# Between two layers of a decoder trunk: the last squares summed on TensorE, the root taken from the sum, a residual in small pieces, the second norm's sums later, and hT normed behind its last reader

## The reference

```
def rmsnorm(x, g):
    y = x * rsqrt(mean(x * x, axis=-1) + 1e-6)
    return y * g

# layer 0 ends with, and layer 1 ends likewise
y = (concat(o_tok, o_mem) * silu(gate)) @ w_o      # 2048 x 2048
x = x + rmsnorm(y, g_post[0])                      # residual

# layer 1 begins with
h = rmsnorm(x, g_pre[1])
p_shift, q_mem, gate = split(h @ w_in)             # r, k, v, two low-rank inputs, memory queries, gate
```

## Time and profile before

| | |
|---|---|
| median of 3 runs | 1711.69 us (1710.7 to 1712.37) |
| the profiled execution's own time | 1713.43 us |
| its span | 1711.8 us |
| PE busy | 1623.2 us, 95% of the span |
| DVE busy | 1049.7 us, 61% |
| ACT busy | 401.3 us, 23% |
| granted TensorE clock, mean | 0.981 of full speed |

### The profile page before, as it was taken

One profiled execution on the slowest core, in us unless ns is written; L12 is line 12 of the kernel. 1 busy time (PEld: TensorE's weight loads), 2 busy tenths in 40 slices (PEclk: granted clock), 3 DMA queues, 4 the chain that ended last, 5 costly groups with the idle time before them and its releaser, 6 DMA issues.

```text
span 1711.8 us, 27852 instructions
## 1 busy us (share of the span) xinstructions
PE 1623.2 (95%) x9596; PEld 1285.7 (75%) x9596; DVE 1049.7 (61%) x4973; ACT 401.3 (23%) x1002; POOL 160.8 (9%) x295
## 2 busy tenths in 40 slices
PE   7999999899999999989989989999999999999995
PEld 6677776677777777657977867777777777888895
DVE  4887546746465555437872467777777777431755
ACT  2131111101121212211111433333333333221011
POOL 1121112112111121220000000000000000020000
PEclk9999999999999999999999999999999999999998
DMA  9689999999999999995433233333333323374441
GB/s 384 235 335 415 411 406 395 384 396 420 405 401 422 417 419 412 366 379 239 148 141 149 103 101 102 103 103 102 103 109 103 103 78 118 111 272 176 148 148 52
DMA packets 101725, 419.95 MB, mean 245 GB/s; under 512 B 41796, under 2 KB 46288, under 8 KB 91984
## 3 DMA queue, kind: packets, MB, share of 16 engines
q0 software_dynamic: 41680, 218.91, 32.1%
q1 hardware_dynamic: 53256, 187.54, 28.9%
q10 hardware_dynamic: 6648, 11.73, 1.8%
HBM read 405.28 MB, written 12.85 MB: 244 GB/s over the span
## 4 chain that ended last, share of the span: by engine, by line
PE 76%; DVE 9%; ACT 6%; DMA 5%; issue 2%; POOLq 0%; POOL 0%; ACTq 0%; DVEq 0%; SPq 0%
PE psum L743 25%; PE psum L1171 11%; PE psum L812 10%; PE psum L794 6%; PE psum L1034 5%; DMA kvr<-in_cv 3%; PE psum L732 3%; PE psum L781 2%; PE psum L1218 2%; DMA kvr<-in_ck 1%; PE psum L1228 1%; PE psum L754 1%; ACT gT L1777 1%; PE psum L769 1%; DVE kvr L1939 1%
## 5 line engine op out<-in xcount | busy, mean ns | idle before, releaser
L1939 DVE CUSTOM_DVE_ANT_0 kvr<-kvr,arena 128x128 f32<-128x128 f32 x1488 | 323.6, 285 | 114.4 <-DMA kvr<-in_ck 114.0
L743 PE MATMUL psum<-hT,wring 128*128 128x264 f32 x1536 | 364.8, 394 | 0.0
L743 PEld LDWEIGHTS psum<-hT,wring 128*128 128x128 f32 x1536 | 291.9, 194 | 67.8 <-issue 19.8
L1171 PE MATMUL psum<-hT,kvr 128*128 128x264 f32 x1152 | 283.0, 391 | 1.8 <-DVE hT L2267 1.8
L1171 PEld LDWEIGHTS psum<-hT,kvr 128*128 128x128 f32 x1152 | 213.5, 191 | 42.3 <-issue 8.9
L794 PE MATMUL psum<-hT,kvr 128*128 128x264 f32 x512 | 121.5, 388 | 0.0
L1939 DVE DVE_READ_ACCUMULATOR2_ANT arena<- 128x1 f32 x1488 | 120.2, 81 | 0.0
L794 PEld LDWEIGHTS psum<-hT,kvr 128*128 128x128 f32 x512 | 94.8, 190 | 15.8 <-issue 0.9
L677 POOL DMA_DIRECT2D kvr<-in_cv x128 | 67.7, 529 | 377.9 <-PE psum L1034 288.2
L1034 PE MATMUL psum<-kvr,arena 128*32 128x384 f32 x1024 | 98.8, 502 | 4.5 <-DMA kvr<-in_cv 4.5
L677 POOL DMA_DIRECT2D kvr<-in_ck x128 | 67.6, 528 | 216.7 <-issue 216.7
(11 more groups left out here) (433 smaller groups left out, 2318.5 us busy)
## 6 DMA issues: line engine op xcount, KB each, us to landing
kvr<-in_ck POOLq DMA_DIRECT2D x128, 768.0 KB, 11.8
kvr<-in_cv POOLq DMA_DIRECT2D x128, 768.0 KB, 11.4
kvr<-in_wrkv SPq DMA_DIRECT2D x12, 3072.0 KB, 11.9
kvr<-in_wo SPq DMA_DIRECT2D x14, 2048.0 KB, 8.3
wring<-in_wkv SPq DMA_DIRECT2D x12, 2048.0 KB, 11.8
wring<-in_wm SPq DMA_DIRECT2D x8, 2048.0 KB, 12.5
wring<-in_wg SPq DMA_DIRECT2D x8, 2048.0 KB, 12.0
kvr<-in_wg SPq DMA_DIRECT2D x8, 2048.0 KB, 8.8
```

Of the source, the lines that this page charges most:

```text
L743: last = mm(psum[:, m % 2, 0:n], w[:, k, t * P:(t + 1) * P], rhs[:, k, 0:n], start=(k == 0), stop=(k == KT - 1))
L1171: last = mm(psum[:, m % 2, 0:T], w[:, k, t * P:(t + 1) * P], hT[:, k, :], start=(k == 0), stop=(k == KT - 1))
L1939: last = v_.tensor_tensor_reduce(page, page, qb[:, n % 2, h * P:(h + 1) * P], 1.0, 0.0, ALU.mult, ALU.add, S[:, n % 2, j * FH + h:j * FH + ...
```

## The change

Seven edits, all between the layers.

- The squares of the last two tiles are no longer added into `acc0` by DVE. PE adds them in PSUM: one product of ones with `acc0` (tiles 0 to 13) and one with each of the two `sq0` buffers, all accumulated into A.
- The root is taken by ACT directly from A, with 1/D as scale and epsilon as bias (a new two-column tile `eps`), and DVE takes the reciprocal of the root. `rsx` moves to the place of `acc0`. A Sqrt of one `eps` column stands ahead of tile 14 on ACT.
- The residual goes in eight pieces of 1, 1, 2, 2, 2, 4, 2 and 2 row tiles, and ACT signals every row tile of `hT` by itself. `lora_tiles` waits for each k.
- The sums of tile 15 (`output_sums(0, 15)`) move behind the fifth piece. The two steps of the second norm that stood before the residual move behind it. The three sums on PE for the second norm move into `lora_tiles`, behind k = 13.
- The low-rank tiles go to PSUM banks 6 and 7, so that the first two query tiles need not wait for their eviction.
- `hT` is multiplied by the second inverse root while the fourth query tile is computed: rows 0 to 3 when that tile has passed k = 3, and so on, and rows 12 to 15 when it is done. Its eviction comes behind that.
- Counts of `h_out` follow (SP's wait ahead of the `s0` loads becomes 28), and the late units' semaphores take the names of `g_full`, which frees names for the new ones.

```
+        RESIDUAL = [(0, 1), (1, 2), (2, 4), (4, 6), (6, 8), (8, 12), (12, 14), (14, 16)]
+        SUMS_LEFT = 5
...
-            sp.wait_ge(sem("h_out"), 16)
+            sp.wait_ge(sem("h_out"), 28)
...
-            def lora_tiles(after):
+            def lora_tiles():
                 pe.wait_ge(sem("w_full0"), 32)
-                for t in range(2):
-                    pe.wait_ge(sem("p_free"), M_LORA + t + 1)
+                pe.wait_ge(sem("y_out"), 2 * FEW0)
                 for k in range(KT):
-                    if k % 4 == 0:
-                        pe.wait_ge(sem("h_out"), after + k // 4 + 1)
+                    pe.wait_ge(sem("h_out"), 8 + k + 1)
                     for t in range(2):
...
-                        last = mm(psum[0:LORA, m % 2, 0:T], w[:, k, :], hT[:, k, :], start=(k == 0), stop=(k == KT - 1))
+                        last = mm(psum[0:LORA, 6 + t, 0:T], w[:, k, :], hT[:, k, :], start=(k == 0), stop=(k == KT - 1))
...
+                    if k == KT - 3:
+                        for n, (out, total) in enumerate(((B, accg), (Wp, accx), (Xp, accxx))):
+                            pe.wait_ge(sem("n_acc"), min(n + 4, 5))
+                            mm(out[:, 0:T], ones, total, start=True, stop=True).then_inc(sem("n_ss"), 1)
...
-                    pe.wait_ge(sem("p_free"), m + 1)
+                    pe.wait_ge(sem("p_free"), m + 1 if t >= 2 else M_LORA + 2)
                     for k in range(KT):
...
+                        if t == 3 and k in (3, 7, 11):
+                            last.then_inc(sem("q_read"), 1)
...
-            for n, (out, total) in enumerate(((A, acc0), (B, accg), (Wp, accx), (Xp, accxx))):
-                pe.wait_ge(sem("n_acc"), min(n + 3, 5))
-                mm(out[:, 0:T], ones, total, start=True, stop=True).then_inc(sem("n_ss"), 1)
-            lora_tiles(8)
+            pe.wait_ge(sem("n_acc"), 3)
+            mm(A[:, 0:T], ones, acc0, start=True, stop=False)
+            for n in range(2):
+                pe.wait_ge(sem("n_sq"), 2 + n + 1)
+                last = mm(A[:, 0:T], ones, sq0[:, n, :], start=False, stop=n == 1)
+            last.then_inc(sem("n_ss"), 1)
+            lora_tiles()
...
             for n in range(16):
+                if n == 14:
+                    ac(eps[:, 1:2], eps[:, 1:2], ACT.Sqrt)
                 output_tile(0, n)
-            act.wait_ge(sem("n_ms"), 3)
-            ac(rsx, inv2, ACT.Sqrt).then_inc(sem("n_rt"), 1)
-            for c in range(4):
-                act.wait_ge(sem("x_new"), c + 1)
-                for k in range(4 * c, 4 * c + 4):
-                    last = ac(hT[:, k, :], xT[:, k, :], ACT.Copy, scale=gpre(1)[:, k:k + 1])
-                last.then_inc(sem("h_out"), 1)
-            act.wait_ge(sem("n_ms"), 4)
+            act.wait_ge(sem("n_ss"), 3)
+            ac(rsx, A[:, 0:T], ACT.Sqrt, scale=1.0 / D, bias=eps[:, 0:1]).then_inc(sem("n_rt"), 1)
+            for n, (k0, k1) in enumerate(RESIDUAL):
+                act.wait_ge(sem("x_new"), n + 1)
+                for k in range(k0, k1):
+                    ac(hT[:, k, :], xT[:, k, :], ACT.Copy, scale=gpre(1)[:, k:k + 1]).then_inc(sem("h_out"), 1)
+            act.wait_ge(sem("n_ms"), 3)
...
-            dve.wait_ge(sem("n_ss"), 3)
-            ch.do(ts(inv2, A[:, 0:T], 1.0 / D, RMS_EPS, ALU.mult, ALU.add))
-            v_.reciprocal(inv2, inv2).then_inc(sem("n_ms"), 1)
-            dve.wait_ge(sem("n_ms"), 3)
+            dve.wait_ge(sem("n_rt"), 3)
+            ch.do(v_.reciprocal(rsx, rsx))
+            for n, (k0, k1) in enumerate(RESIDUAL):
+                if n == SUMS_LEFT:
+                    output_sums(0, 15)
+                residual(k0, k1, rsx).then_inc(sem("x_new"), 1)
+            ch.do(tt(inv2, rsx, rsx, ALU.mult))
             dve.wait_ge(sem("n_ss"), 6)
             ch.do(tt(prx, inv2, B[:, 0:T], ALU.mult))
             ch.do(tt(prx, prx, Xp[:, 0:T], ALU.add))
-            dve.wait_ge(sem("n_rt"), 3)
-            for c in range(4):
-                residual(c, rsx).then_inc(sem("x_new"), 1)
...
             for t in range(4):
+                if t == 3:
+                    for c in range(4):
+                        if c < 3:
+                            dve.wait_ge(sem("q_read"), c + 1)
+                        else:
+                            dve.wait_ge(sem("p_done"), M_QM1 + 4)
+                        rows4 = hT[:, 4 * c:4 * c + 4, :]
+                        tt(rows4, rows4, inv2.unsqueeze(1).to_broadcast([P, 4, T]), ALU.mult).then_inc(sem("h_out"), 1)
                 dve.wait_ge(sem("p_done"), M_QM1 + t + 1)
                 stt(qT1[:, t, :], psum[:, (M_QM1 + t) % 2, 0:T], SCALE, inv2, ALU.mult, ALU.mult).then_inc(sem("p_free"), 1)
-            for c in range(4):
-                rows4 = hT[:, 4 * c:4 * c + 4, :]
-                tt(rows4, rows4, inv2.unsqueeze(1).to_broadcast([P, 4, T]), ALU.mult).then_inc(sem("h_out"), 1)
```

More of the change, by code:

```diff
@@ L275, in trunk_step @@
         ptc = sb("ptc", [P, 1], I32)
+        eps = sb("eps", [P, 2])
         arena = sb("arena", [P, AR])
@@ L375, in trunk_step @@
         acc0, accg, accx, accxx, prx, inv2 = (re.take(T) for _ in range(6))
-        rsx = sq0[:, 0, :]
+        rsx = acc0
         rm = Region(qb[:, 1, :], PAGE_W)
@@ L468, in few_slot, with late_full @@
             return (v - PLAIN0) % 3 if layer == 0 else (v + 8) % 3
+        def late_full(v):
+            return sem(f"g_full{v % 3}"), (48, 48, 32)[v % 3] + 16 * (v // 3 + 1)
         def few_full(i):
@@ L472, in few_full @@
             return (sem(f"g_full{few_slot(i)}"), 16 * ((v - PLAIN0) // 3 + 1 + (few_slot(i) < 2))) if layer == 0 else \
-                (sem(f"u_full{few_slot(i)}"), 16 * ((v + 8) // 3 + 1))
+                late_full(v + 8)
         def few_weights(i):
@@ L630, in late_unit @@
                 sp.wait_ge(sem("p_done"), M_G1 - 3 if v == 0 else M_G1 if v < 3 else M_G1 + 2 * (v - 3) + 2)
-                sp.dma_start(gunit[:, v % 3, :], I["wg1"][G1_UNITS[v]] if v < 8 else I["wo1"][v - 8]).then_inc(sem(f"u_full{v % 3}"), 16)
+                sp.dma_start(gunit[:, v % 3, :], I["wg1"][G1_UNITS[v]] if v < 8 else I["wo1"][v - 8]).then_inc(sem(f"g_full{v % 3}"), 16)
             for o in range(-1, RP - 1):
@@ L789, in late_part @@
                     if t == 0:
-                        pe.wait_ge(sem(f"u_full{v % 3}"), 16 * (v // 3 + 1))
+                        pe.wait_ge(*late_full(v))
                     pe.wait_ge(sem("p_free"), m + 1)
@@ L1168, in project_part @@
                     if o == -2 and t == 0:
-                        pe.wait_ge(sem("h_out"), 12 + n + 1)
+                        pe.wait_ge(sem("h_out"), 24 + n + 1)
                     for k in range(4 * (n % 4), 4 * (n % 4) + 4):
@@ L1425, in output_tile @@
                     act.wait_ge(sem("sq_used"), nth - 1)
-                ac(sq[:, j % 2, :], oT[:, n, :], ACT.Square)
+                last = ac(sq[:, j % 2, :], oT[:, n, :], ACT.Square)
+                if layer == 0 and j >= 14:
+                    last.then_inc(sem("n_sq"), 1)
                 ac(oT[:, n, :], oT[:, n, :], ACT.Copy, scale=gpost(layer)[:, n:n + 1]).then_inc(sem("p_free"), 1)
@@ L1797, in _ @@
                 output_tile(1, n)
-            root(4, rs1)
+            root(3, rs1)
             for c in range(4):
@@ L2107, in few_units @@
                     joined(i)
-                for j in (14, 15):
+                for j in (14, 15) if layer else (14,):
                     output_sums(layer, j)
@@ L2129, in output_sums @@
                 s, total = (sq0, sq1)[layer][:, j % 2, :], (acc0, acc1)[layer]
-                last = v_.tensor_copy(total, s) if j == 0 else tt(total, total, s, ALU.add)
+                if layer or j < 14:
+                    last = v_.tensor_copy(total, s) if j == 0 else tt(total, total, s, ALU.add)
                 if layer:
@@ L2134, in output_sums @@
                     return
-                if j == 15:
+                if j == 13:
                     last.then_inc(sem("n_acc"), 1)
@@ L2151, in output_sums, with residual @@
                         ch.do(last)
[L2153 to L2156, removed]
+            def residual(k0, k1, buf):
+                rows_ = slice(k0, k1)
+                ch.do(tt(oT[:, rows_, :], oT[:, rows_, :], buf.unsqueeze(1).to_broadcast([P, k1 - k0, T]), ALU.mult))
+                return tt(xT[:, rows_, :], xT[:, rows_, :], oT[:, rows_, :], ALU.add)
+            v_.memset(eps[:, :], RMS_EPS)
             quad, total = oT[:, 0:4, :], oT[:, 4:8, :]
@@ L2255, in _ @@
                 dve.wait_ge(sem("p_done"), M_LORA + t + 1)
-                tt(pb[0:LORA, t, 1:T + 1], psum[0:LORA, (M_LORA + t) % 2, 0:T], inv2[0:LORA], ALU.mult).then_inc(sem("p_free"), 1)
+                tt(pb[0:LORA, t, 1:T + 1], psum[0:LORA, 6 + t, 0:T], inv2[0:LORA], ALU.mult).then_inc(sem("p_free"), 1)
             dve.wait_ge(sem("p_free"), M_LORA + 2 + 2)
@@ L2468, in _ @@
             for c in range(4):
```

(2 more changed lines are left out.)

1 line of the change is left out of this document (removed).

## The result

| | before | after |
|---|---|---|
| median of 11 runs each, taken together | 1711.69 us (1706.42 to 1718.26) | 1702.59 us (1697.06 to 1707.69) |
| profiled execution, own time | 1713.43 us | 1697.31 us |
| span | 1711.8 us | 1695.6 us |

A forecast was written before the change was run, and what follows sets the result against it. PE, busy 95% of the span, was taken as the bound, so removed standstills pay: restart 6.0 gained, sums 1.3 and clock and feed 0.8 paid, bank 0.5 and tail 2.0 gained. 1711.7 - 6.4 = 1705.3 us, range 1703.3 to 1708.3.

The forecast's parts named there:

- The front: From layer 0's last join to PE's restart on the low-rank tiles: restart at 892.4 instead of 898.39, 6.0 us earlier.
- rival 1: ACT's Sqrt table lacks Square, so a table load returns before the root: 0.9 us later, total 1706.2; chance 8%.
- The tail: End of the queries to the first projection: hT multiplied during the fourth query tile removes the 2.0 us there.
- 0.8 paid for clock and feed: Low-rank tiles: loss to half clock and late residual pieces, 2.1 against the old order's 1.45, rounded.
- 1.45 lost: Half clock lasting 2.9 us after the old restart at 898.39, of which PE loses half.
- 2.1 lost: Half-clock loss after the new restart, taken as the middle of two restarts seen; puts k = 8 at 901.6.
- The bank move: Low-rank tiles in other PSUM banks: the queries' wait for their eviction goes, 0.5 us gained.
- all later work starts from that last one: The first projection's start, 938.6 instead of 945.03, was taken to set all later work: 6.4 us earlier.
- Theory A: Stated with the experiments: the gain is the 6.6 us from last product to first projection; other differences are clock chance.
- theory B: Stated with the experiments: the change also keeps the clock from falling in the recurrence's first turn, about 3 us more.
- Rival 3: Layer 1 gives gain back through further clock falls, 1.5 to 2.7 us each; total 1709; chance 6%.
- The range: Forecast interval for the total, 1703.3 to 1708.3 us; the forecast's own bounds, 1703.7 to 1706.9, used 0.9 for run spread.

The follow-up runs named there:

- e9: The kernel before, unchanged, run again: 0.4 ± 0.9 us above the kernel before, ratio 1.0005.
- e7: The kernel before with four products of ones with constants in PE's standstill in the recurrence's first turn: 2.4 ± 1.0 us below the kernel before, ratio 0.9985.
- e5: The changed kernel, unchanged, six more runs: 10.3 us below the kernel before, ratio 0.9936.
- e13: The changed kernel, unchanged, a third time, six runs: 9.7 us below the kernel before, ratio 0.9938.
- e6: The changed kernel with four products of ones with constants in PE's standstill in the recurrence's first turn: 8.2 ± 1.6 us below the kernel before, ratio 0.9946.
- e8: The changed kernel with tile 15's sums behind the sixth residual piece instead of the fifth: 6.9 ± 1.3 us below the kernel before, ratio 0.996.
- e4: The changed kernel with PE's standstills before the restart and in the first turn filled, tile 15's sums behind the sixth piece: 11.2 ± 1.7 us below before, ratio 0.9932.
- e12: Second test of the changed kernel with both PE standstills filled and tile 15's sums behind the sixth piece: 11.7 ± 1.1 us below the kernel before, ratio 0.9931.
- e11: The changed kernel with mean and reciprocal on DVE ahead of ACT's root, squares still on PE: 6.9 ± 1.0 us below the kernel before, ratio 0.9957.
- e3: The changed kernel with the residual in four pieces of four row tiles, tile 15's sums behind the second: 5.8 ± 1.0 us below the kernel before, ratio 0.9963.
- e1: The changed kernel with hT again multiplied after the fourth query tile's eviction, as before: 4.0 ± 1.0 us below the kernel before, ratio 0.9977.
- e2: The kernel before with only hT's multiply moved into the fourth query tile: 2.5 ± 1.1 us below the kernel before, ratio 0.9982.
- e10: The changed kernel with the low-rank tiles back in PSUM banks 0 and 1: 2.1 ± 0.9 us below the kernel before, ratio 0.9984.
- e14: The changed kernel with eight products of ones with constants in PE's standstill before the restart: 10.1 ± 1.3 us below the kernel before, ratio 0.9944.
- e15: The changed kernel with PE's standstill before the restart filled and tile 15's sums behind the sixth piece: 11.5 ± 1.7 us below the kernel before, ratio 0.9935.

## Where the gain comes from, and why the forecast was short

**The stretch, over all executions of either order** (before, e9, e7; after, e5, e13, e6, e8), in us:

| | old order | mean | new order | mean | forecast, old to new |
|---|---|---|---|---|---|
| last product to restart | 11.60, 11.68, 11.68 | 11.65 | 5.68, 5.67, 5.68, 5.67, 5.67 | 5.67 | -6.0 |
| restart to queries | 16.14, 17.63, 17.19 | 16.99 | 17.31, 18.31, 17.31, 18.16, 17.31 | 17.68 | +1.6 |
| queries to projection | 30.50, 30.50, 30.50 | 30.50 | 28.48 in all five | 28.48 | -2.0 |
| sum | | 59.14 | | 51.83 | -6.4 |

- The front: right, 6.0. So were the steps in it, and no table load came back: Square ran with the Sqrt's table, at 879.54 behind the load at 869.13. The Trainium skill (ScalarE: Activation LUTs, "Table sets: the hidden batching unit") doesn't name Square among what every set holds, which was the ground for rival 1. After that load the next instruction starts 1.29 us from the load's start. The 2.66 us that the Trainium skill has for a switch (same page, "What ACT_TABLE_LOAD costs") doesn't show here.
- The tail: right, 2.0, and none of DVE's work behind it was late.
- The low-rank tiles: the step "0.8 paid for clock and feed" is the term that was mis-sized. It held one execution of the old order (1.45 lost, the mildest of those since seen) against a middle for the new. Over all executions the old order loses as much as the new: 16.99 - 0.55 = 16.4 without the wait for the bank, against 17.68 - 1.33 = 16.4 without the sums. So the term measured 0. By the clock's record the 2.1 lost that I took for the new order was right, 2.1 in the mean of five; it was the old order's 1.45 that was too small, 2.3 in the mean of three (half clock behind the restart for 2.9, 5.9 and 5.0 us). The two figures differ by 0.65, not 0.8; the sum had rounded. In all, the term is 0.9 of what was missing.
- The bank move: its effect is in the sum, but the working gave it 0.5 where it now prevents 5.5.
- After the stretch the working had nothing: "all later work starts from that last one". From the first projection to the end, the old order took 766.8 and 766.3 (before, e9), the new 763.7, 765.1, 765.5 and 765.9 (after, e5, e13, e8). That is 1.4 us more in the means, and 7.3 + 1.4 = 8.7 stands beside 9.6 ± 0.9 measured. Half of the time at half clock in that part, wherever it fell (the last 17 us aside, where every execution falls), is 3.4 and 1.7 us against 0, 1.7, 1.7 and 1.7, means of 2.6 and 1.3. So the 1.4 is the clock's, as far as six executions can tell; that the change brings it isn't shown. The kernel with both fills can be set up the same way: its stretch is 9.0 shorter than the old order's, and it has no half clock behind it, 2.6 less: 11.6, beside 11.6 ± 0.9 measured (e4 and e12 together).

**The first turn.** Theory A said chance, theory B that the change keeps the clock. Both were put too simply. A pattern shows when the executions with a fall at the front and no fill are set in order of the distance from the clock's rise behind the restart to PE's next start in the turn's standstill (the rise from the trace's record of the granted clock, the start from its timeline):

| execution | distance, us | at half clock in the first turn, us |
|---|---|---|
| e5, after | 82.79, 83.01 | none, none |
| e13, e8, e11 | 83.06, 83.06, 83.09 | 3.4 each |
| e9 | 83.57 | 3.4 |
| e3 | 83.77 | 3.4 |
| e1, before | 84.72, 85.10 | 6.8 each |

The order holds whichever kernel it is: e9 is the kernel before and falls like e8; e1 has the new front and falls like before. So the fall isn't tied to an edit. But the distance is, in part. PE's work behind the rise is the same in every execution of one order, and the change alters it: without the 2 us of the tail's standstill, and with the sums inside, the distance is 82.8 to 83.1 in all five executions of the new order (e6, with its fill, would have 83.0), and 83.6 to 85.1 in the three of the old (e7, with its fill, would have 84.0). The new order lands in the cheaper part, but close to its edge: between none (83.01) and 3.4 us (83.06) lie 0.05 us.

The length of the distance alone doesn't decide. e2 with 81.84 and e10 with 68.04, where other work lies between, fell for 6.8 each, though both are shorter than e5's. In e14 and e15 the front fill moved the last rise far ahead: 208.50 us and no fall, 227.53 and 6.8. That the distance causes the fall, and isn't only beside it, was argued from this table and from the fills (2.4 ± 1.0 gained in the old order, none in the new). It wasn't tried by shifting one kernel's distance alone. With so few executions the share of this in the gain, at most the 1.4 us above, stays rough.

Rival 3 had the right mechanism, a clock fall elsewhere in layer 1, with the wrong sign: I had it as a loss only. The range was too narrow on two grounds: three runs' spread was taken for the kernel's, and a term bounded from one execution was held against a median. The first median lies 0.7 us outside the range, less than its error of 1.4; the 9.6 of all 23 runs lies outside by 1.2, with an error of 0.9. So that the first result fell outside is partly luck, and the two terms above are what the forecast lacked.

## What to carry to other kernels

A standstill of PE has two prices: its length, and the clock behind it. Where PE resumes short of data, a short fall of the clock and a late feed cover each other, so look at both before removing one. When one edit makes a result come later (here the second norm's sums), look again at every wait that hung on it: the buffer that cost 0.5 us before would cost 5.5 in the new order. And compare lengths between instants of the same stage, over several executions, before a difference of totals is explained.

## What was not expected of the hardware

- A wait of 3.8 us in the midst of dense work cost 5.5: 3.8 itself and 1.8 for the clock behind it (e10).
- A standstill of 2.2 us in dense work cost 0, 3.4 or 6.8 us at half clock in executions with the same instructions around it. Among the nine executions of the table the outcome went with the distance from the clock's last rise: none at 83.01, 3.4 at 83.06, 6.8 at 84.72.
- Products of ones with constants, written over later and read by nobody, kept the clock at full in every profiled execution that had them (e4, e6, e7, e12, e14, e15 at the places they filled), and delayed PE's restart by nothing.
